# A second Strassen stage, quartered norm sums and another order of the recurrent mixer in a three-layer block kernel

## The reference

```python
def _rms_norm(x, g):
    y = xf * lax.rsqrt(jnp.mean(xf * xf, axis=-1, keepdims=True) + EPS)
    return (y * g.astype(jnp.float32)).astype(x.dtype)
...
def _swiglu(h, w_in, w_out):
    gate, up = jnp.split(h @ w_in, 2, axis=-1)
    return (jax.nn.silu(gate) * up) @ w_out
...
        x = x + g1 * y
        x = x + g2 * _swiglu(_modulate(_rms_norm(x, norm_ffn[i]), sh2, sc2), ffn_w_in[i], ffn_w_out[i])
...
    kk = kk / jnp.maximum(jnp.sqrt(jnp.sum(kk * kk, axis=-1, keepdims=True)), 1e-12)
    k = k * (1.0 + (a - 1.0) * k_a)
...
    y = ((y - mean) * lax.rsqrt(var + GN_EPS)).reshape(B, S, RWKV_W) * ln_w + ln_b
    bonus = (jnp.sum(r_h * k_h * r_k, axis=-1, keepdims=True) * v_h).reshape(B, S, RWKV_W)
    return ((y + bonus) * g).astype(p_shift.dtype)
```

## Time and profile before

| | us |
|---|---|
| median of 3 runs | 2105.18 (2102.28 to 2107.67) |
| the profiled execution, its time | 2107.79 |
| its span, first to last instruction | 2106.0 |
| PE busy | 1994.2 |
| DVE busy | 813.9 |
| ACT busy | 283.5 |
| POOL busy | 235.0 |

### The profile page before, as it was taken

How to read it: one execution, slowest core, us unless ns; L and a number is a source line. 1 busy time by engine, 2 the same in 40 slices (tenths; PEclk the granted TensorE clock), 3 DMA queues, 4 the chain that set the end, 5 groups by cost and what they waited for, 6 DMA issues and landing times.

```text
span 2106.0 us, 24100 instructions
## 1 busy us (share of the span) xinstructions
PE 1994.2 (95%) x10014; PEld 1273.3 (60%) x10014; DVE 813.9 (39%) x1376; ACT 283.5 (13%) x593; POOL 235.0 (11%) x242
## 2 busy tenths in 40 slices
PE   6999889999999989989899999989988999999998
PEld 2444338888854464447788888768877545555444
DVE  2556345888842044264334213665342200000001
ACT  2000020000000021143100002242112100000000
POOL 0001013555500020000011001210000000000000
PEclk9999999999999999999999998999998999999999
DMA  9423413554451261001877443221025799999997
GB/s 398 170 87 101 158 60 120 165 166 162 129 209 70 80 260 40 0 1 61 359 260 255 153 168 148 100 105 62 3 82 238 294 426 428 429 428 428 429 428 318
DMA packets 48776, 420.14 MB, mean 199 GB/s; under 512 B 5440, under 2 KB 5456, under 8 KB 22960
## 3 DMA queue, kind: packets, MB, share of 16 engines
q1 hardware_dynamic: 29376, 344.73, 40.4%
q0 software_dynamic: 18880, 71.18, 10.1%
q10 hardware_dynamic: 432, 2.96, 0.4%
HBM read 417.81 MB, written 1.05 MB: 199 GB/s over the span
## 4 chain that ended last, share of the span: by engine, by line
PE 78%; DVE 11%; DMA 7%; ACT 2%; issue 2%; DVEq 0%; ACTq 0%; SPq 0%; POOLq 0%
PE PS L971 11%; PE PS L1143 9%; PE PS L1271 8%; PE PS L913 8%; PE PS L984 5%; DVE SC L1653 5%; DMA ring<-w_moe 5%; PE PS L1326 4%; PE PS L1131 4%; PE PS L946 4%; PE PS L1292 4%; PE PS L1305 3%; PE PS L1101 2%; PE PS L1004 2%; PE PS L1112 2%
## 5 line engine op out<-in xcount | busy, mean ns | idle before, releaser
L971 PE MATMUL PS<-A,ring 128*128 128x512 f32 (+1 forms) x704 | 228.5, 486 | 1.1 <-DVE A L1764 1.1
L1143 PE MATMUL PS<-ring,A 128*64 128x512 f32 x1024 | 223.4, 593 | 3.7 <-DMA ring<-w_moe 2.9
L971 PEld LDWEIGHTS PS<-A,ring 128*128 128x128 f32 x704 | 133.4, 190 | 95.7 <-issue 85.3
L1271 PE MATMUL PS<-A,ring 128*128 128x512 f32 x384 | 168.3, 599 | 2.0 <-ACT A L549 2.0
L1143 PEld LDWEIGHTS PS<-ring,A 128*64 128x64 f32 x1024 | 73.9, 137 | 149.9 <-issue 141.7
L1653 DVE SCALAR_TENSOR_TENSOR SC<-A,CS,SC 128x512 f32<-128x512 f32 x208 | 161.9, 833 | 6.0 <-DMA A<-ada 4.0
L946 PE MATMUL PS<-A,ring 128*128 128x256 f32 x704 | 159.3, 388 | 3.5 <-ACT A L549 3.5
L946 PEld LDWEIGHTS PS<-A,ring 128*128 128x128 f32 x704 | 136.0, 194 | 27.0 <-issue 8.2
L913 PE MATMUL PS<-ring 128*128 128x256 f32 x672 | 151.1, 381 | 0.0
L913 PEld LDWEIGHTS PS<-ring 128*128 128x128 f32 x672 | 126.9, 190 | 25.3 <-issue 8.5
L1271 PEld LDWEIGHTS PS<-A,ring 128*128 128x128 f32 x384 | 73.0, 191 | 96.8 <-issue 94.9
(11 more groups left out here) (338 smaller groups left out, 2263.1 us busy)
## 6 DMA issues: line engine op xcount, KB each, us to landing
ring<-w_moe SPq DMA_DIRECT2D x96, 2048.0 KB, 18.2
ring<-w_fin SPq DMA_DIRECT2D x44, 1024.0 KB, 6.9
ring<-ada POOLq DMA_DIRECT2D x64, 512.0 KB, 3.9
A<-ada POOLq DMA_DIRECT2D x64, 512.0 KB, 4.0
ring<-w_fout SPq DMA_DIRECT2D x16, 1408.0 KB, 6.1
ring<-w_conv SPq DMA_DIRECT2D x8, 1536.0 KB, 11.9
ring<-w_qkv SPq DMA_DIRECT2D x6, 2048.0 KB, 16.0
ring<-w_win SPq DMA_DIRECT2D x6, 2048.0 KB, 10.7
```

The source lines that it names most:

```text
L971: mm = pe.matmul(PS[:, s, 0:T], slot(stage, s, k * 128, k * 128 + 128), HID[:, k * T:(k + 1) * T], start=(k == 0), stop=(k == KF - 1))
L1143: mm = pe.matmul(PS[CAP * e:CAP * (e + 1), g, :], XG[:, k * P + e * CAP:k * P + (e + 1) * CAP], slot("moe", k // 2, w, w + 512), start=(k ...
L1271: mm = pe.matmul(PS[:, 3 * (j % 2) + c, :], slot("conv", j, k * 384 + c * 128, k * 384 + c * 128 + 128), h_of(k, 512), start=(k == 0), sto ...
```

## The change

Three parts, in one diff.

1. `fout0` by the same recursion, in four pairs of feature blocks: per pair 7 products of 11 matmuls with 256 columns. DVE makes four sums of the hidden activations (`FT`, 2816 columns each), once; POOL makes four sums of the weights for each pair (`FS`, 1408 columns each), DVE puts the products together (five tensor_tensor and four scalar_tensor_tensor for a pair).
2. The sums of the six norms, and of the two norms over heads, are quartered: four matmuls with 32 output partitions each put a quarter of the tokens (or a pair of heads) into a quarter of the partitions; root and reciprocal work on a quarter of the columns; a second product (`norm_spread`, `head_spread`) with a column of the identity as weights spreads the result over all partitions into PSUM, from where DVE reads it. For n = 0 the spread stands after `ada_columns`. POOL's second `fold_weights` waits for the end of the norm.
3. The mixer's order: kk is normed earlier, exponentials get their own buffer (EN), gates 1 and 2 stand ahead of the transposes, gate 3 between the levels, gate 4 between the chunk steps, gate 5 around the norm over heads and gates 6 and 7 behind it; gate and bias of the output are applied ahead of time.

```diff
-    ("fout0", 8, 2816, 4, 1),
+    ("fout0", 8, 2816, 4, 2),
...
+FOLD_T, FOLD_S = 11264, (18304, 19712, 16896, 21120)
...
+        HID4 = HID[:, 0:KF * 512].rearrange("p (k s t) -> p k s t", k=KF, s=2)
+        FT = [A[:, 0:2816].rearrange("p (k t) -> p k t", k=11),
+              ring[:, FOLD_T:FOLD_T + 2816].rearrange("p (k t) -> p k t", k=11), HID4[:, 0:11, 0, :],
+              ring[:, FOLD_T + 2816:FOLD_T + 5632].rearrange("p (k t) -> p k t", k=11)]
+        FS = [ring[:, o:o + 1408].rearrange("p (k m) -> p k m", k=11) for o in FOLD_S]
...
+                elif s == 2:
+                    pool.wait_ge(sem("h_ready"), HB[1] + 2 * KD)
...
+            def fold_out(i, third):
+                w0 = slot("fout0", 2 * i, 0, 2816).rearrange("p (k m) -> p k m", k=KF)
+                w1 = slot("fout0", 2 * i + 1, 0, 2816).rearrange("p (k m) -> p k m", k=KF)
+                a11, a12, a21, a22 = w0[:, 0:11], w0[:, 11:22], w1[:, 0:11], w1[:, 11:22]
+                done = MMB["fout0"] + 4 * (i - 1)
+                n = 84 + 4 * i
+                if third:
+                    pool.wait_ge(sem("product"), done + 4 if i else MMB["fin0"] + 3 * 22)
+                    pool.tensor_tensor(FS[2], a11, a21, ALU.subtract).then_inc(sem("pool_made"), 1)
+                    return
+                slot_landed(pool, "fout0", 2 * i)
+                slot_landed(pool, "fout0", 2 * i + 1)
+                pool.wait_ge(sem("product"), done + 3 if i else MMB["fin0"] + 3 * 20)
+                pool.tensor_tensor(FS[0], a21, a22, ALU.add).then_inc(sem("pool_made"), 1)
+                pool.wait_ge(sem("pool_made"), n + 1)
+                pool.tensor_tensor(FS[1], FS[0], a11, ALU.subtract).then_inc(sem("pool_made"), 1)
+                pool.wait_ge(sem("pool_made"), n + 2)
+                pool.tensor_tensor(FS[3], a12, FS[1], ALU.subtract).then_inc(sem("pool_made"), 1)
+            fold_out(0, False)
+            group_loads(None, PG_BASE[1] + 10, range(2, 4))
+            fold_out(0, True)
+            group_loads(None, PG_BASE[1] + 11)
+            for i in range(1, 4):
+                fold_out(i, False)
+                fold_out(i, True)
...
-                act.activation(RN[:, 0:T], PS[:, 7, 0:T], ACT.Sqrt, bias=eps, scale=1.0 / D).then_inc(
+                act.wait_ge(sem("stat_done"), 2 * n + 1)
+                act.activation(RN[:, 0:T // 4], PS[:, 7, 0:T // 4], ACT.Sqrt, bias=eps, scale=1.0 / D).then_inc(
...
+            def norm_sums(n):
                 T = NORMS[n][2] * SEQ
+                w = T // 4
                 for k in range(KD):
                     pe.wait_ge(sem("sq_done"), 8 * n + k + 1)
-                    mm = pe.matmul(PS[:, 7, 0:T], ones, SQ[:, k * T:(k + 1) * T], start=(k == 0), stop=(k == KD - 1))
+                    for t in range(4):
+                        mm = pe.matmul(PS[32 * t:32 * t + 32, 7, 0:w], ones[:, 0:32], SQ[:, k * T + t * w:k * T + (t + 1) * w],
+                                       start=(k == 0), stop=(k == KD - 1))
                 mm.then_inc(sem("stat_done"), 1)
+            def norm_spread(n):
+                w = NORMS[n][2] * SEQ // 4
+                pe.wait_ge(sem("inverted"), n + 1 + (2 if n == 5 else 0))
+                for t in range(4):
+                    mm = pe.matmul(PS[:, 7, t * w:(t + 1) * w], ident[:, 32 * t:32 * t + 1].to_broadcast([P, P]), RN[:, 0:w],
+                                   start=True, stop=True)
+                mm.then_inc(sem("stat_done"), 1)
+            def norm(n):
+                norm_sums(n)
+                norm_spread(n)
...
+            def head_sums(src, bank):
+                for m in range(4):
+                    mm = pe.matmul(PS[32 * m:32 * m + 32, bank, 0:SEQ], bo64[:, 48:80], src[:, m * SEQ:(m + 1) * SEQ],
+                                   start=True, stop=True)
+                return mm
+            def head_spread(src, b0):
+                for m in range(4):
+                    for h in range(2):
+                        o = 32 * m + 16 * h
+                        mm = pe.matmul(PS[64 * h:64 * h + 64, b0 + m // 2, (m % 2) * SEQ:(m % 2) * SEQ + SEQ],
+                                       con("ident", o, o + 1).to_broadcast([P, 64]), src[:, 0:SEQ], start=True, stop=True)
+                return mm
...
+            def ffn_out_folded():
+                def fold(bank, half, left, right):
+                    for k in range(11):
+                        mm = pe.matmul(PS[:, bank, half * 256:half * 256 + 256], left[:, k], right[:, k],
+                                       start=(k == 0), stop=(k == 10))
+                    return mm
+                for i in range(4):
+                    slot_landed(pe, "fout0", 2 * i)
+                    w0 = slot("fout0", 2 * i, 0, 2816).rearrange("p (k m) -> p k m", k=KF)
+                    w1 = slot("fout0", 2 * i + 1, 0, 2816).rearrange("p (k m) -> p k m", k=KF)
+                    b = 3 * (i % 2)
+                    if i < 2:
+                        pe.wait_ge(sem("folded"), 4 + 5 * (20 + i))
+                    else:
+                        pe.wait_ge(sem("folded"), 113 + 5 * (i - 1))
+                    pe.wait_ge(sem("ffn_act"), 42 + i if i == 0 else 43 + i)
+                    fold(7, i % 2, w0[:, 0:11], HID4[:, 0:11, 1, :]).then_inc(sem("product"), 1)
+                    if i == 0:
+                        pe.wait_ge(sem("hid_done"), 24)
+                    fold(b + 1, 1, w0[:, 11:22], HID4[:, 11:22, 1, :])
+                    pe.wait_ge(sem("pool_made"), 84 + 4 * i + 4)
+                    fold(b, 0, FS[3], HID4[:, 11:22, 0, :])
+                    if i == 0:
+                        pe.wait_ge(sem("folded"), 113)
+                    fold(b + 1, 0, FS[1], FT[1]).then_inc(sem("product"), 1)
+                    slot_landed(pe, "fout0", 2 * i + 1)
+                    if i < 3:
+                        fold(b, 1, w1[:, 11:22], FT[3])
+                        fold(b + 2, 0, FS[0], FT[0]).then_inc(sem("product"), 1)
+                        fold(b + 2, 1, FS[2], FT[2]).then_inc(sem("product"), 1)
+                    else:
+                        fold(b + 2, 0, FS[0], FT[0])
+                        fold(b + 2, 1, FS[2], FT[2]).then_inc(sem("product"), 1)
+                        pe.wait_ge(sem("folded"), 113 + 5 * 3)
+                        fold(0, 0, w1[:, 11:22], FT[3]).then_inc(sem("product"), 1)
+                    if i < 2:
+                        ada_sum(1, 10 + i)
+                ada_spread(1)
...
+            pe.wait_ge(sem("kk_sq"), 1)
+            head_sums(BB, 6).then_inc(sem("kk_stat"), 1)
             for m in range(4):
                 dst = PS[:, 4 + m // 2, (m % 2) * 256:(m % 2) * 256 + 256]
                 pe.matmul(dst, slot("lora", 0, 512 + m * 128, 640 + m * 128), RP[:, 256:512], start=True, stop=False)
                 mm = pe.matmul(dst, slot("lora", 0, 1024 + m * 128, 1152 + m * 128), RP[:, 512:768], start=False, stop=True)
             mm.then_inc(sem("product"), 1)
-            gate_part(1, 6, 0, 2 * KD)
-            pe.wait_ge(sem("kk_sq"), 1)
+            pe.wait_ge(sem("gate_sig"), 1)
+            gate_part(1, 7, 0, 10)
+            pe.wait_ge(sem("inverted"), 6)
+            head_spread(RNK, 0).then_inc(sem("kk_stat"), 1)
+            gate_part(1, 7, 10, 2 * KD)
+            pe.wait_ge(sem("kk_root"), 1)
+            gate_part(2, 6, 0, 8)
+            pe.wait_ge(sem("mixer_step"), 3)
             for b in range(2):
-                mm = pe.matmul(PS[:, b, :], bo64, BB[:, b * 512:(b + 1) * 512], start=True, stop=True)
-            mm.then_inc(sem("kk_stat"), 1)
-            pe.wait_ge(sem("gate_sig"), 1)
-            gate_part(2, 7, 0, 2 * KD)
-            pe.wait_ge(sem("mixer_step"), 2)
-            for b in range(2):
-                mm = pe.matmul(PS[:, 2 + b, :], bo64, EE[:, b * 512:(b + 1) * 512], start=True, stop=True)
+                mm = pe.matmul(PS[:, 2 + b, :], bo64, RKP[:, b * 512:(b + 1) * 512], start=True, stop=True)
             mm.then_inc(sem("rk_sum"), 1)
-            for m in range(3, 5):
-                pe.wait_ge(sem("gate_sig"), m - 1)
-                gate_part(m, 7 - m % 2, 0, 2 * KD)
+            gate_part(2, 6, 8, 2 * KD)
...
+                if 1 <= lv < 5:
+                    gate_part(3, 7, 4 * lv - 4, 4 * lv - 2)
                 if lv:
                     for b in range(2):
                         level_second(lv, b)
+                if 1 <= lv < 5:
+                    gate_part(3, 7, 4 * lv - 2, 4 * lv)
...
-            gate_part(6, 4, 0, KD)
+            gate_part(5, 4, 0, 4)
             pe.wait_ge(sem("y_copied"), 1)
             for b in range(2):
                 mm = pe.matmul(PS[:, b, :], bo64, YY[:, b * 512:(b + 1) * 512], start=True, stop=True)
             mm.then_inc(sem("mean_sum"), 1)
-            gate_part(6, 4, KD, 2 * KD)
+            gate_part(5, 4, 4, 10)
             pe.wait_ge(sem("var_sq"), 1)
             pe.wait_ge(sem("state"), NCH)
-            for b in range(2):
```

(29 more changed lines are left out.)

212 lines of the change are left out of this document (128 added, 84 removed).

## The result

| | us |
|---|---|
| before, median of 4 runs | 2106.34 (2102.28 to 2107.67) |
| changed, median of 4 runs | 2077.60 (2073.88 to 2078.63) |
| ratio, 95% interval | 0.9866 (0.9847 to 0.9885) |
| changed, a second set of 4 runs | 2076.98, ratio 0.9868 (0.9851 to 0.9884) |
| changed, the profiled execution, its span | 2073.88, 2072.1 |

Faster by 28.7 us; the forecast was 2077. The profiled execution of the changed kernel is its shortest, 3.7 under its median, and the one of before 1.5 above its own, so the two traces differ by 33.9.

The account below looks back on a forecast made before the run. PE product chain bounds it to about 1630 us, then the experts' weight stream; earlier savings move the end one for one. Folded output +2, norms -20, mixer -10: -28 from 2107.8, less 2.6 to the median, 2077; range 2062 to 2096.

Parts of the forecast that it names:

- What bounds the kernel: Whole kernel: PE chain up to about 1630 us, then experts' weight stream; PE savings before 1630 move the end one for one.
- The folded output: First block's output, fout0: products -18.6, first-pair stall +17.5, clock +3; net +2, bounds -7 and +9.
- the turns with DVE: First pair of fout0: up to three DVE FT sums, 9.3 us, push POOL's weight sums behind.
- The norms: All six norms: quartered sums, root and reciprocal save 20 us in sum, bounds -12 and -25.
- The second norm (n = 1) has its last squares about 1.5 later relative to its sums: -5.1: Second norm: narrow sums and shorter reciprocal gain 5.1 us, against 5.9 for the third, because its last squares come later.
- the other term: Second norm: with the third operand from PSUM, DVE stops taking turns with POOL, 9.51 to 6.42, -3.1 us.
- behind it the PE waits 4.05 for DVE's ada group, so its gain is swallowed: 0: Fourth norm (n = 3): no gain, because the PE's wait for DVE's ada group behind it absorbs the saving.
- rival 4: Narrow norm records cost 219 ns each instead of 35, making the kernel slower, 2147 us; chance 0.03.
- The mixer: Reordered gates, earlier kk norm and quartered head sums in the mixer: -10 us, bounds -13 and -5.
- of which it fills waits like the 2.38: -2.5: Mixer levels: gate 3, placed between them, costs 6.9 us but hides 2.5 of it in PE waits.
- Rival 1: First stall short since FT and FS don't take turns, clock stays up at norms: -42, 2063 us; chance 0.20.
- Rival 2: POOL's sums cost 3.5 us each and the mixer's order gives little: -14, 2091 us; chance 0.17.

Follow-up runs that it names:

- pairs kernels: Three edits of the changed kernel reordering the products of fout0's first pair, or of all pairs, to follow their sums: 2065.33, 2063.74 and 2061.43 us.
- sums_in_turn: Changed kernel, with DVE beginning its four FT sums only after POOL has ended its four sums of the first pair: 2082.35 us.
- gate3_front: Changed kernel with gate 3 as one piece ahead of the transposes instead of eight pieces between the levels: 2074.53 us, ratio 0.9836.
- pairs_best: Changed kernel: all pairs reordered, first two product by product, POOL's second-pair sums before the ada loads, DVE's FT1 after POOL's first sum, one ada sum moved: 2061.43 us.
- pair_order2: Changed kernel; in the first pair PE takes each product once its own sums are ready, DVE makes FT3 before FT2: 2065.33 us, ratio 0.9801.

## Why the prediction was right, and where it was not

The time was 2077.6 against a forecast of 2077, well inside the range, but the terms beneath it were not all as good as their sum.

**What bounds the kernel** held: what was saved ahead of the experts' stage moved the end one for one, since no stage behind it gave anything back. From the experts' first product to the end it is 464.5 before and 464.2 after, and 464.0 to 465.0 in all 13 traces. The pairs kernels, 12 to 16 us shorter again, say the same.

**The folded output** was right in size and in mechanism. 151.6 to 132.9 of products; a stall of 17.59 against 17.5; 2.7 of clock behind it (22 records in 7.5 instead of 4.75, at a granted clock of 0.64) against 3. Slot 1 was ready 6.2 after the stage's start, against 6.3. Two terms in the stall were off and cancelled: a sum of POOL takes 3.15, not 2.6 (2.24 ns a column, between the two rows; I had taken the lower end since its width was nearer, and the truth was nearer the middle), +2.2; and the turns with DVE cost 7.3, not 9.3, since the first of POOL's sums and a part of the last ran free. That the two take turns, which the short operations of the earlier trace rows hinted at, is seen in every row there and disappears in sums_in_turn. The Trainium skill's rule ("SBUF — State Buffer", section "Who interferes with whom"), an exclusive hold on the shared ports for a whole instruction, agrees with these rows: 5.88 is 2.73 of wait and 3.15 of work.

**The norms** were 5.6 better than forecast (-25.5 against -19.9), and two steps of them failed. The first, for n = 1 (-10.7 against -8.2): "The second norm (n = 1) has its last squares about 1.5 later relative to its sums: -5.1". In the trace after, the last square does end late, 1.65 behind the start of the sums against 0.72 in n = 2; but in n = 2 a table load of 1.28 stands behind it, and here none, so that the root starts 2.2 behind the start of the sums, and 2.0 in n = 2. The lateness costs next to nothing: from the start of the sums to the next product it is 6.4 instead of 13.8, -7.4 where I had -5.1. About 1.0 of the 7.4 is a turn with POOL, which I had put into the other term (DVE's second piece took 1.48 before); the products behind it are another 3.4 shorter, against 3.1 for all the turns. The second, for n = 3: "behind it the PE waits 4.05 for DVE's ada group, so its gain is swallowed: 0". The wait is still 3.59, but DVE's group begins behind an addition that waits for the PE's products, and so comes forward with them: it begins 17.9 and 16.6 behind the start of the norm's sums in the two traces with the old norm, 16.4 in the changed kernel. The gain was kept: 0.7 to 2.0, by which of the two old traces is taken. The +0.6 for reading the spread from PSUM did not come (6.36 against 6.42). Narrow records cost 30 ns with 128 columns (35 taken) and 22 with 64; rival 4, at 219, was far off.

**The mixer** was 3.6 worse (-6.4 against -10). The step that failed is "of which it fills waits like the 2.38: -2.5". Gate 3 between the levels cost 6.6 of its 6.9 (1.1 ahead of the levels and 5.5 in them): it shortened that one wait by 1.06 and took away two of 0.40, but its eight pieces cost 1.5 more than the 6.9 of one piece. Apart from the 1.38 ahead of the chunk steps, which stayed, the 31 us of the levels held no other wait on the PE above 0.05. gate3_front shows the same from the other side. I had taken one idle row as a sample of many. Chunk steps +1.4 (1.0), the tail +1.7 (1.0), the front -14.2 (-14.5), the branch -1.8 (-1.9) were near.

**The rivals.** Rival 1 (a short stall) is what pairs_best brings about by its order, 2061 against the 2063 worked out for it; the changed kernel itself does not. Rival 2's dear POOL sum was half true (3.15) but no later pair stalled: the second pair's four sums ended at 638.2 where the PE needed them at 640.1, 2 us to spare. In pair_order2 the PE came there 15 us sooner after the stage's start and POOL's sums only 10, which made the wait of 3.21.

## What to carry to other kernels

Count for an algorithmic saving when its first use can start: here 18.6 us of products saved were paid back in full by a step that waited for the last of four sums although one of its products needed only the first. Let an engine wait for the operand it uses next and order its work as the operands are made; that brought 16 us of them back. Two engines that take turns on memory can be kept apart by putting one operand in PSUM, which costs nothing where a product makes it there anyway. Before a piece of work is moved to "fill waits", add up the idle rows of the place it is moved to.

## What the hardware did that I had not expected

The clock of one stretch differs between executions of the same program: of 13 profiles, 9 had the first five lora records in 2.50, three in 1.34 and one in 1.55, right behind the same wait of 2.3 to 2.4 for w_lora; over the first 12 us the granted clock is 0.61 to 0.62 in the nine, 1.00 in the three and 0.72 in the one, the kernel before. The 12 us at the start of the projections were at 0.72 in the kernel before and at 1.00 in both profiles of the changed one, but this is no work of the change: of the nine other edits of the changed kernel, whose code is the same there, six ran there at 0.77 to 0.78 and three at 1.00. 3 to 4 us each, as much as a whole term of a sum; what picks one or the other I did not find out.

Who waits depends on 0.02 us: POOL's first sum took 3.15 or 6.08 as it began just before or just after DVE's. And the turns are not always one for one: beside a row of short ada sums of DVE, POOL's single sum took 9.08 and ended 3.0 after the last of them, while DVE's ran at full speed (8 in 5.38), as if POOL had been held off for all of them. pairs_best has the same row, 9.08, ending 3.0 behind DVE's last.
